# A down projection in seven products: second sums ahead of deferrable vector work, and the next tile's sums made in the tile in front

## The reference

```python
h = rms_norm(x, ln_mix_pre)
gate_b, gate_c, u, v = split(h @ w_in)              # 4 x 1024 channels
y_conv = head_norm(gate_b * conv3_causal(gate_c * u))
y_pool = head_norm(pooled(v) @ pool_w) * pool_scale
x = x + rms_norm(concat(y_conv, y_pool) @ w_out, ln_mix_post)
hf = rms_norm(x, ln_ffn_pre)
g, up = hf @ w_gate, hf @ w_up                       # 2048 -> 5632
ff = (silu(g) * up) @ w_down                         # 5632 -> 2048
x = x + rms_norm(ff, ln_ffn_post)
```

## Time and profile before

| what | before |
|---|---|
| median of 3 runs | 2520.8 us (2519.39 to 2520.86) |
| the profiled execution | 2521.66 us |
| its span, slowest core (core 6) | 2518.8 us |
| spans of the 8 cores | 2495.6 to 2518.8 us |
| granted TensorE clock, mean of a core | 0.983 to 0.989 |
| PE busy, core 6 | 2408.2 us, 96% |
| DVE busy / ACT busy, core 6 | 1283.7 / 651.8 us |
| down projection, pass 0: tile 0, tile 1 | from 964 to 1128 us, to 1289 us |
| down projection, pass 1: tile 0, tile 1 | from 2205 to 2347 us, to 2493 us |

### The profile page before, as it was taken

One profiled execution on the slowest core, in us unless ns is written; L12 is line 12 of the kernel. 1 busy time (PEld: TensorE's weight loads), 2 busy tenths in 40 slices (PEclk: granted clock), 3 DMA queues, 4 the chain that ended last, 5 costly groups with the idle time before them and its releaser, 6 DMA issues.

```text
span 2518.8 us, 37768 instructions; the slowest of 8 cores (2495.6 to 2518.8 us)
## 1 busy us (share of the span) xinstructions
PE 2408.2 (96%) x13915; PEld 1340.2 (53%) x13915; DVE 1283.7 (51%) x2002; ACT 651.8 (26%) x1248; POOL 210.3 (8%) x363
## 2 busy tenths in 40 slices
PE   5999999999999999898989999999999999999995
PEld 2444444444444446787854444444444444488885
DVE  3556546445544454437635553474554445454655
ACT  3333344122222221321113333441222222211111
POOL 0000000000000000001101100000000000000121
PEclk8999999999999999999999999999999999999998
DMA  9979779989989896646896534698554455344774
GB/s 227 169 109 134 179 220 169 171 121 133 133 128 133 127 134 213 217 169 184 240 208 110 92 68 167 218 188 152 90 88 84 85 91 90 82 172 150 215 209 121
DMA packets 76085, 377.52 MB, mean 150 GB/s; under 512 B 8320, under 2 KB 10624, under 8 KB 46592
## 3 DMA queue, kind: packets, MB, share of 16 engines
q0 software_dynamic: 52720, 310.93, 62.8%
q1 hardware_dynamic: 23184, 64.19, 7.8%
HBM read 512.44 MB, written 65.01 MB: 229 GB/s over the span
## 4 chain that ended last, share of the span: by engine, by line
PE 87%; DMA 6%; DVE 3%; issue 2%; ACT 1%; SPq 0%; POOL 0%; DVEq 0%; ACTq 0%; POOLq 0%
PE bank L409 85%; DMA unit<-wd_bf 3%; DMA F<-xt 2%; DMA unit<-wst_gu 2%; DVE F L441 1%; DVE XG L444 1%; PE bank L614 1%; DVE tt L441 1%; PE bank L449 1%; PE bank L886 1%; DVE unit L441 1%; DMA unit<-wst_in 0%; DVE XG L441 0%; ACT tt L438 0%; SPq L505 0%
## 5 line engine op out<-in xcount | busy, mean ns | idle before, releaser
L409 PE MATMUL bank<-XG,unit 128*128 128x512 bf16 (+1 forms) x8000 | 1721.9, 376 | 12.1 <-DMA unit<-wst_in 4.1
L409 PEld LDWEIGHTS bank<-XG,unit 128*128 128x128 bf16 x8000 | 784.0, 98 | 929.6 <-issue 27.3
L409 PE MATMUL bank<-F,unit 128*128 128x256 bf16 (+1 forms) x4224 | 514.8, 283 | 19.5 <-DMA unit<-wd_bf 9.5
L409 PEld LDWEIGHTS bank<-F,unit 128*128 128x128 bf16 x4224 | 417.8, 99 | 103.5 <-issue 22.7
L435 ACT ACTIVATE tt<-bank 128x512 f32<-128x512 f32 (+1 forms) x292 | 160.0, 549 | 606.4 <-PE bank L409 593.2
L441 DVE TENSOR_TENSOR bank<-bank,tt 128x512 f32<-128x512 f32 x152 | 106.3, 700 | 356.9 <-PE bank L409 356.9
L441 DVE TENSOR_TENSOR unit<-unit 128x1024 bf16<-128x1024 bf16 x360 | 234.6, 686 | 10.0 <-PE bank L409 2.1
L441 DVE TENSOR_TENSOR tt<-tt 128x512 f32<-128x512 f32 (+1 forms) x151 | 104.1, 692 | 149.3 <-ACT tt L438 125.1
L441 DVE TENSOR_TENSOR tt<-bank,tt 128x512 f32<-128x512 f32 (+1 forms) x108 | 66.2, 613 | 193.3 <-PE bank L409 193.3
L441 DVE TENSOR_TENSOR F<-bank,tt 128x512 bf16<-128x512 f32 (+1 forms) x146 | 98.6, 677 | 126.9 <-PE bank L409 106.0
L357 POOL DMA_DIRECT2D unit<-wst_gu x100 | 52.9, 529 | 1021.1 <-PE bank L409 922.3
(11 more groups left out here) (90 smaller groups left out, 1227.0 us busy)
## 6 DMA issues: line engine op xcount, KB each, us to landing
unit<-wst_gu POOLq DMA_DIRECT2D x100, 1024.0 KB, 11.1
unit<-wd_bf POOLq DMA_DIRECT2D x64, 1024.0 KB, 7.1
unit<-wo_bf POOLq DMA_DIRECT2D x32, 1024.0 KB, 6.3
unit<-wst_in POOLq DMA_DIRECT2D x31, 1024.0 KB, 12.4
unit<-wd_bf POOLq DMA_DIRECT2D x32, 768.0 KB, 5.4
wd_bf<-wst_dn POOLq DMA_DIRECT2D x32, 704.0 KB, 17.3
F<-xt SPq DMA_DIRECT2D x24, 512.0 KB, 33.3
XG<-xt SPq DMA_DIRECT2D x24, 512.0 KB, 8.1
```

The lines of the kernel that those rows point to most:

```text
L409: inst = e.matmul(out, lhsT=pairs[n][0], rhs=pairs[n][1], start=(start and n == 0), stop=(stop and n == nk - 1), skip_group_check=lax)
```

## The change

Four things are changed in the down projection, and the same computation is done.

1. Within groups 1 to 7 the group's own squares and adds (`late`, `close`) and `side` of the group in front are now emitted behind the next group's first product, its copy s1 and its second sum. Before, they stood ahead of these.
2. The first sums of tile 1, and its T(0) and T(1), are emitted at the end of tile 0 (`nxt.sums`, `nxt.t12`). For that T and SQ of pass 0's tile 1 move to F0 blocks 16 to 39 and 8 to 15. Tile state is kept in the class `DnTile`.
3. In group 0 PE's list has the product c += quad 1 x B(1, 0) ahead of b and a's second products (it was behind them), and in the three tiles with nS = 2 the direct part of b is taken forward.
4. At the end of pass 0 `done(u2)` no longer emits a load (`finished.add(u2)`), so that the fifth `wst_in` load is issued during the next stage. The chunk buffer F0 8 becomes F0 40.

```diff
+            def sums(self, s, u):
+                S1, K1 = self.SQ(u, 0)
+                S2, K2 = self.SQ(u, 1)
+                tt(S1, quad4(s, 2), quad4(s, 3), ALU.add, [("U", s, 2), ("U", s, 3)], K1)
+                tt(S2, S1, quad4(s, 0), ALU.subtract, K1 + [("U", s, 0)], K2)
+                tt(quad4(s, 2), quad4(s, 0), quad4(s, 2), ALU.subtract, [("U", s, 0), ("U", s, 2)], [("U", s, 2)])
...
+            def t12(self):
+                self.tsum(self.Tb(0), self.B(0, 1), self.B(0, 0))
+                self.tsum(self.Tb(1), self.B(1, 1), self.Tb(0))
...
-            nun = [use_unit("dn") for _ in US]
-            for u in US:
-                sums(slot_of[nun[u]], u)
-            tsum(T(0), B(0, 1), B(0, 0))
-            tsum(T(1), B(1, 1), T(0))
...
                 for u in US:
+                    tt(quad4(ss[u], 0), quad4(ss[u], 1), SQ(u, 1)[0], ALU.subtract, [("U", ss[u], 1)] + SQ(u, 1)[1], [("U", ss[u], 0)])
                 if first:
+                    cf.tsum(B(0, 1), B(1, 1), B(0, 1))
+                    cf.tsum(T(2), B(1, 0), T(1))
+                else:
+                    close()
+                    side(c2 - 1)
...
+                more = cf if c2 < 7 else nxt
+                if more is not None:
+                    ns = more.ask()
+                    more.sums(ns[0], 0)
...
                 tt(o0[:, HT:TT], banks[b.i][:, 0:HT], snv[2], ALU.add, [b, h2], k0)
-                side(c2)
-                plain(a, slot_of[u2], 32, 12, 1, 0, False)
-                done(u2)
+                plain(a, slot_of[u2], 1, 0, False)
+                if more is nxt and nxt is None and cur["p"] == 0:
+                    finished.add(u2)
+                else:
+                    done(u2)
                 act_copy(o1[:, 0:HT], banks[a.i][:, 0:HT], [a], k1)
-                for o, k in ((o0, k0), (o1, k1)):
-                    acc.square(o, k)
-                    acc.add()
-            return acc
+                late += [(o0, k0), (o1, k1)]
+                if c2 == 7:
+                    if nxt is not None:
+                        nxt.t12()
+                    close()
+                    side(7)
+            return acc, ns
```

More of the change, by code:

```diff
@@ L1091, in build_program @@
         HT = TT // 2
-        def dn_tile(par, side, apart=False):
-            p = cur["p"]
-            acc = Acc(KC, apart=apart)
[L1096 to L1100, removed]
-            snv = (Tt[9][:, 0:HT], Tt[9][:, HT:TT], xhalo[:].rearrange("p a b -> p (a b)"))
[L1102 to L1128, removed]
-                S1, K1 = SQ(u, 0)
-                S2, K2 = SQ(u, 1)
-                tt(S1, quad(s, 2), quad(s, 3), ALU.add, [("U", s, 2), ("U", s, 3)], K1)
-                tt(S2, S1, quad(s, 0), ALU.subtract, K1 + [("U", s, 0)], K2)
-                tt(quad(s, 2), quad(s, 0), quad(s, 2), ALU.subtract, [("U", s, 0), ("U", s, 2)], [("U", s, 2)])
@@ L1135, in prod, with quad4, dn_tile @@
+        def quad4(s, n):
+            return units[s][:, 1024 * n:1024 * n + 1024]
+        def dn_tile(cf, nxt, ss, side, apart=False):
+            par, F, nS, h9 = cf.par, cf.F, cf.nS, cf.h9
+            B, T, SQ = cf.B, cf.Tb, cf.SQ
+            US = range(nS)
+            acc = Acc(KC, apart=apart)
+            snv = (Tt[9][:, 0:HT], Tt[9][:, HT:TT], xhalo[:].rearrange("p a b -> p (a b)"))
             def prod(bank, lhs, rhs, start):
@@ L1155, in snap, with plain @@
+            def plain(bank, s, e2, half, start):
+                w = units[s][:, 0:12 * 256].rearrange("p (k n) -> p k n", n=256)
+                mm_group(bank, lambda k: w[:, k, e2 * 128:(e2 + 1) * 128], lambda k: F[:, 32 + k, half * HT:(half + 1) * HT], range(12),
+                         reads=[Kffa(par, 32 + k) for k in range(12)] + KU(s), ncols=HT, start=start, lax=not start)
             def snap(n, bank):
                 h = P.alloc("sn", n)
-                extra = first_use.pop(n, [])
@@ L1175, in dn_tile, with close @@
-            nun = [use_unit("dn") for _ in US]
-            for u in US:
-                sums(slot_of[nun[u]], u)
-            tsum(T(0), B(0, 1), B(0, 0))
-            tsum(T(1), B(1, 1), T(0))
+                act_copy(snv[n], banks[bank.i][:, 0:HT], [bank] + ([h9] if n < 2 else ["xhalo"]), [h])
+                return h
+            late = []
+            def close():
+                for o, k in late:
+                    acc.square(o, k)
+                    acc.add()
+                late.clear()
@@ L1417, in side_d0 @@
                     nx["bufs"] = [load_chunk(2, k, b4[k]) for k in range(4)]
-            acc = dn_tile(0, side_d0)
+            h9 = P.alloc("t", 9)
+            hs = [P.alloc("t", i) for i in (1, 4, 5, 6)] if p else None
+            cf = [DnTile(0, h9, hs), DnTile(1, h9, hs)]
+            s0 = cf[0].ask()
+            for u in range(cf[0].nS):
+                cf[0].sums(s0[u], u)
+            cf[0].t12()
+            acc, s1 = dn_tile(cf[0], cf[1], s0, side_d0)
             tl0 = Tail(te, acc)
@@ L1433, in side_d1 @@
                     nx_to(c2)
-            acc = dn_tile(1, side_d1, p == 1)
+            acc, _ = dn_tile(cf[1], None, s1, side_d1, p == 1)
             if p == 0:
```

137 lines of the change are left out of this document (75 added, 62 removed).

## The result

The change takes the time from 2520.8 us to 2488.3 us (medians of four runs each). Some executions of every kernel here, before and after alike, take longer at a lower granted clock on one die or both (2606.1 us at 0.94 in one of these four, 2909.4 us at 0.83 before and 2928.2 us at 0.82 after in the runs of c0), and the ratios, and the medians from here on, leave them out. That gives 2520.8 and 2485.9 us, a ratio of 0.9866 with a 95% interval of 0.9839 to 0.9892. The forecast was 2492 us, worked out for the profiled execution, which took 2485.9 us.

What follows compares the result with a forecast made beforehand. PE, busy 96% of the span, was taken as the bound, so only its standstills and lowered clock could be won: 13.4 + 0 + 5.5 + 4.7 + 6.2 = 29.8 us off 2521.66, forecast 2492 us, range 2483 to 2508.

Steps and rivals of the forecast that it cites:

- Tile 1 of pass 0: Down projection: second sums made first and ch1 loaded ahead of the stores win 13.4 of 15.4 us lost.
- I take 2 us as still lost: Tile 1 of pass 0: allowance for transfers falling behind, leaving 13.4 us won of 15.4.
- a backlog of 1.5 us a group: Tile 1, groups 1 to 4: 19.0 us of DMA per 17.47 us of PE, 6 us behind in all.
- Rival 1: Tile 1, pass 0: transfers are the bound; 7 us or nothing won there, 2498 or 2505 us; chance 0.12.
- Tile 0: Pass 0: squares delay copy s5, so four PE waits for ACT sum to 9.8 us, for 9.7 before; 0 us won.
- The boundaries: Tile 0 to tile 1: sums of tile 1 made early win 5.5 us in pass 0, 4.7 in pass 1.
- From pass 0 to pass 1: Factor at L490 no longer waited for, but a later chunk of x costs 2 us, clock 1; 6.2 us won.
- the 27.8 us of the earlier trace: Start of pass 1: assumed landing time of the last chunk of x, putting it 17.9 us into the stage.
- the equal packet counts of the earlier trace: End of pass 0, 1269 to 1289 us: POOL's queue 432 packets, SP's 425, read as agreeing with packet turns.
- Rival 2: Tile 0, pass 0: late chunks of x stop ACT, 10 us more in four groups, about 2532 us; chance 0.03.
- Rival 3: Second sums or T(0) also wait for a unit on its way; gain under 5 us, about 2518; chance 0.04.
- Rival 4: Stages that become dense: PE's clock falls to 0.81, two tiles cost 60 us, 2552 us; chance 0.01.

Runs made afterwards that it cites:

- c0: The unmodified change run a second time, beside the kernel before on another chip; ratio to before 0.9855.
- e1: The change with side and the own squares and adds ahead of the second sums again, ch1 load behind the stores again; ratio to before 0.9892.
- e3: The change with DVE's new order kept, but the ch1 load issued behind the four accumulating stores; ratio to before 0.9983.
- e7: The change with tile 0's sixteen rows finished and stored over six groups instead of four; ratio to before 0.9879.
- e4: The change with tile 1's first sums, T(0) and T(1) made at tile 1's start again; ratio to before 0.9885.
- e6: The change with the fifth wst_in load at its old place, the end of pass 0; one run, 2488.1 us.
- e9: The change with side(7) ahead of the last own adds in tile 1 of pass 0, fifth load still late; one run, 2491.6 us.
- e2: The change with DVE's old order, the ch1 load kept ahead of the accumulating stores; ratio to before 0.9911.
- e5: The change with side, in tile 0 of pass 0, behind copy h2 and the add on bank a; ratio to before 0.9827.

## Why the prediction was right

**The sum.** 29.8 us of gain were forecast and 35.8 measured between the profiled executions (2491.9 and 2485.9 us); the main mechanism and its place were right, and the four terms that were to bring the gain all did. Two terms were mis-sized, tile 0 and the start of pass 1, by 9.0 us together in the table above. That the sum misses by less is in part luck: the other terms came out 4.0 us below the forecast, 2.2 of it at a weight load that the change doesn't touch.

*Tile 1 of pass 0* (13.4 forecast, 12.3 measured). e1 to e3 show that the order on DVE and the load's place both count. The second sums come when forecast, and the moved work ends 0.9 us ahead of DVE's next duty (0.6 forecast). "I take 2 us as still lost" was 3.1 on core 7 and 2.3 on the mean of the cores (0.9 in c0), as a wait for ch2 in group 5, which is where a backlog of 1.5 us a group should show. The landing times under e7 show this backlog at 1.8 us a group in the change and 1.4 in c0. Rival 1 is thus true in kind, but at about the 2 us that the forecast allowed for, not at 6 or 13. What the prediction didn't see is how unequal the two links are: that the load's place carries nearly all, and that without it the new order on DVE would have made the tile slower than before (156.1 us in e3 for 147.0 in e1).

*Tile 0* (0 forecast, 5.2 measured). This is the term that failed, and by its own test ("I am wrong if tile 0 changes by more than 4 us"), though not by much: on the mean of eight cores the tile gained 4.1 us (4.9 in c0). The mechanism was right: four waits, for s5, of 1.0, 1.75, 3.4 and 1.75 us against 1.4, 2.2, 4.0 and 2.2. Each is 0.4 to 0.6 us shorter than worked out. ACT in time, core 7 after:

```profile
1029.02 0.63 ACT L438 ACTIVATE tt<-XG 128x512 bf16<-128x512 f32 x1 [0.23 <-DVE tt L441]
1029.56 0.36 ACT L435 ACTIVATE tt<-bank 128x256 f32<-128x256 f32 x1
```

The last of the ten squares starts about 6.8 us into the group, for 7.2 worked out, and the copy starts 0.54 us after it, where I had let the square's whole 0.63 us pass. That makes 2 us of waits; the other 3 were clock. The longest wait, 3.4 us for 4.4, was followed by 40 matmuls in 6.19 us, 1.7 more than after the other three waits, where before it was 2.7 (8 matmuls in 1.87 us and 56 in 8.19). The first 48 matmuls of the tile lost 1.3 us, where the first 40 before had lost 2.7, behind a wait of the same length; this part belongs to the two profiles and not to the change. I had set the clock's part equal on both sides without a row for it.

*The boundaries* (5.5 and 4.7 forecast, 5.5 and 4.0 measured). Right within 1 us. e4 shows that half or more came from the product taken forward, which the prediction had named only as cover.

*From pass 0 to pass 1* (6.2 forecast, 10.0 measured). The last chunk's load was issued 7.3 us into group 7 (7.5 forecast). Its landing is the step that failed: I carried the 27.8 us of the earlier trace rows over, a single load on a single core.

```profile
1268.55 0.69 DVE L441 TENSOR_TENSOR tt<-tt 128x512 bf16<-128x512 f32 x1 [0.17 <-DVE tt L441]
...
1280.47 0.75 DVE L444 SCALAR_TENSOR_TENSOR XG<-F,constsb,tt 128x512 bf16<-128x512 f32 x1 [5.94 <-DMA F<-xt]
```

On core 7 it was 24.2 us (issued at 1256.26), on five of eight cores the chunk was not waited for at all, and the matmul at 1287.30 did not wait. I also did not see a second wait in this stage: on cores 1, 2, 5 and 7 of the kernel before PE never waited at L490, but lost up to 5.6 us later, for the stores of tile 0's rows. e6 shows that issuing the fifth load late is what removed this; the prediction had given that part of the change no gain.

**On the queues.** The forecast took from the Trainium skill (DMA: Bandwidth & Descriptors, "Queues, rings and completion order") that the queues are served a packet in turn, so that one load less in POOL's queue doesn't speed SP's. e6 and e9 agree with it on core 6, 25.2 us with the load and without it, as far as one core can. But the equal packet counts of the earlier trace rows did not come back: from 1249 to 1269 us of the change they are

```profile
q0 software_dynamic: 370, 2.57, 80.1%
q1 hardware_dynamic: 623, 1.28, 21.0%
```

so that equality was no proof of turns, and no run here shows how the engines pick between the queues; the shares of time (80 and 17 to 21%) are what stayed.

**The rivals.** Rival 2 (late chunks stop ACT in tile 0): ACT never waited for a DMA there, on any core. Rival 3 (second sums or T(0) wait for a unit): PE waited for neither on any core. Rival 4 (the clock falls when the gaps close): the granted clock is 1.00 over 85 dense us, and the mean of the slowest core rose from 0.983 to 0.987. The Trainium skill's 13/16 (TensorE: Matmul & The Clock Gate, Part 1) is again not seen in the profiled execution, with eight busy cores.

## What to carry to other kernels

When vector work is moved out of the way of a critical operation, look at what else was issued behind it: here the weight load that stood behind four stores on the same queue carried some 10 to 20 us, and the order on DVE, once the load was in time, 1 to 2. The stores waited for DVE, and an engine that issues in order holds a load back behind them. In-order engines that hand buffers to each other (squares on ACT, adds on DVE, four buffers) are best given their work where they are idle in the middle of a group; put ahead of a copy that frees PE's bank, every square is on PE's path (e2, e5). And when a queue is full at a stage's end, issuing the transfer that is needed last behind the ones that are needed first can be worth several us of waiting, 2.4 to 5.8 here, though the queue moves no less (e6).

## What the runs showed of the hardware that was not expected

A load of 1 MB that takes a median of 6.5 us with only weights and chunks of x under way (`unit<-wd_bf`, tile 0 of pass 0) takes 13 to 19 us in tile 1's groups with stores. Issued behind the four accumulating stores it took 13.8 to 15.0 us (before, means of eight cores); issued ahead of them it took 9.4 us in the first group and 13.4, 15.1 and 16.8 in the next three (the change). So its place in the queue didn't count for how fast it landed: it counted because POOL, which issues in order, stood waiting for the data of the stores. With four stores in every group the time to landing grew by 1.4 to 1.8 us a group, close to the 1.5 worked out from the busy shares of the DMA engines, and with three it didn't grow at all (e7). PE without a single gap for 85 us at a DMA share of 0.94 shows that nearly full DMA engines need not cost the matmuls anything, as long as each load is issued earlier than its growing time to landing; on core 7 the wait came 3.4 us after these 85.
